# The first norm's weight: a partition-spreading DMA replaced by one row and two TensorE products

## The chip, the cores and the metric

The kernel runs on one core of one Trainium2 chip. The metric is the device time of the whole kernel in microseconds, the median of several runs. The lines of this document (L930 and so on) are lines of the kernel before, unless a sentence says that they are of the changed one.

## The reference

A conditioning vector `c` modulates two mixer layers, and two blocks with gated feed-forward layers follow. What matters here is the very start: the modulation and the norm of layer 0, ahead of the first projection.

```python
def adaln_norm(x, c, g, w_ada, b_ada):
    mod = jax.nn.silu(c) @ w_ada + b_ada
    shift, scale, gate = jnp.split(mod, 3, axis=-1)
    h = rms_norm(x, g) * (1.0 + scale[:, None, :]) + shift[:, None, :]
    return h, gate[:, None, :]
...
    for i in range(DEPTH):
        h, gate = adaln_norm(x, c, norm_g[i], ada_w[i], ada_b[i])
...
            y = nsa_mixer(h, nsa_w_in[j], ...)
```

`x` is 256 tokens by 1024, `c` is 1 by 1024, `g` is a row of 1024 and `w_ada` is 1024 by 3072, all float32. The rest (two mixers, the output projections, the feed-forward layers, further norms) isn't touched by the change.

## The kernel before

Each engine has its own block of instructions in a fixed order written by hand, and semaphores tie the blocks together. Tokens lie on the 128 partitions in two tiles (`NT = 2`); `x` and `tok` are 128 x 2 x 1024.

**The start.** SyncE issues the large loads from one queue, in this order: `x` (1 MB), the four halves of the first two blocks of `ada_w0` (1 MB each, tiles `early_111` to `early_114`, "early"), the first half of the first `nsa_w_in` item (716 KB, into `ring`), then further blocks as earlier ones are used. ScalarE issues two small loads at its start: `c`, and the identity matrix (64 KB, into `tab`). GpSimd sets constants, issues the load of vector 0 (`load_vec(0)`, the weight `norm_g[0]`), then the load of `ada_b` (12 KB, one row, into `mod0`).

`vecs` in HBM has one row of 1024 for each of eleven norm vectors. `load_vec(v)` copies row v to all 128 partitions with `partition_broadcast`: 512 KB written for 4 KB of data, into one of the two halves of the tile `vec`.

**Modulation, block by block.** `EARLY = (2, 0, 3, 1)`: TensorE makes four blocks of 512 columns of `silu(c) @ w_ada`, first half of scale, first half of shift, then the second halves. The weights are the moving operand, and `cb` (128 x 32, silu(c) in column 0) the stationary one. One block is two halves of four products (L1339), into four 32-partition strips of a PSUM bank. VectorE adds the bank to `mod0` (L2402), TensorE multiplies with `ones` to sum the partitions and spread the result to all 128 (L1350), and VectorE takes it: for a scale block as `(scale + 1) * g` (L2411, `scale_gain`, which reads `vec`), for a shift block in the last step of the norm (L2422). The normed tokens are transposed on TensorE (L528) into banks `T0`/`T1` and copied out as a high part (ScalarE, L538) and a low part (VectorE, L569). `keep_busy(n, ...)` (L1132) is n products without use, which TensorE works on while it would otherwise wait. From then on TensorE multiplies with split weights, high and low parts (`whi` from ScalarE, `wlo` from VectorE), in the three products of L1109 to L1111.

A float32 product of 128 x 512 shows in the trace as two MATMUL records; those of L1109 to L1111 show as one each.

Of the kernel before, what the change touches and what calls it, by code (L numbers as in the profile page):

```python
# [128 lines left out]
def two_stacks(nc, a, out):  # L129
    with ExitStack() as ctx:  # L130
        def sem(name):
            return ctx.enter_context(nc.semaphore(name))

        def stage(name, names):
            return Signals(ctx, nc, name, names)
# [5 lines left out]
        def sb(name, shape, dt=F32, over=None, skip=0):  # L141

            size = -(-4 * int(np.prod(shape[1:])) // 32) * 32
            if over is None:
                place[name] = at_byte[0]
                at_byte[0] += size
                assert at_byte[0] <= nc.sbuf_top, (name, at_byte[0], nc.sbuf_top)
            else:
                place[name] = place[over] + skip
            return nc.alloc_sbuf_tensor_at(name, list(shape), dt, offset=place[name])  # L150
# [32 lines left out]
        vec = sb("vec", [P, 2, D])  # L183
# [13 lines left out]
        ones = sb("ones", [P, P])  # L197
# [15 lines left out]
        TB = [ctx.enter_context(nc.psum_tensor(f"T{i}", [P, 512], F32)) for i in range(2)]  # L213
# [55 lines left out]
        vec_loaded, vec_used = [sem("vec0_loaded"), sem("vec1_loaded")], sem("vec_used")  # L269
# [3 lines left out]

        early_landed = [sem(f"early{m}_landed") for m in range(4)]
        near_landed, near_scaled = [sem("near0_landed"), sem("near1_landed")], sem("near_scaled")
        gains_loaded = sem("gains_loaded")
        early, late = stage("ada_early", "part summed full taken"), stage("ada_late", "part summed full taken")
        norm = stage("norm", "var rstd ready half resid squared meaned mean centered")
        turn = stage("turn", "turned taken low drawn")
# [188 lines left out]
        def plan_turn(name, groups, split=False):  # L468

            turns[name] = (groups, *turn_n, split)  # L470
            turn_n[0] += len(groups)
            turn_n[1] += sum(len(takes) for g, (_, takes) in enumerate(groups) if name not in SHARED or g % 2 == 0)
            turn_n[2] += len(groups) if split else 0
# [8 lines left out]
        def wait_turned(eng, name, upto=None):  # L482

            groups, _, t0, _, _ = turns[name]
            n = len(groups) if upto is None else upto
            eng.wait_ge(turn["taken"], t0 + (n + 1) // 2)
            eng.wait_ge(turn["drawn"], drawn0[name] + n // 2)

        def turned_all(name):

            groups, _, t0, l0, split = turns[name]
            return (turn["low"], l0 + len(groups)) if split else (turn["taken"], t0 + sum(len(takes) for _, takes in groups))
# [22 lines left out]
        def turn_pe(pe, name, ready=None, tile=None, only=None):  # L515
            groups, _, t0, l0, split = turns[name]
            for g, (srcs, takes) in of_tile(groups, tile) if only is None else ((only, groups[only]),):
                if ready is not None:
                    ready(g)
                if name in SHARED and g >= len(banks_of(name)):  # L520

                    free = (g - len(banks_of(name))) // 2 + 1
                    pe.wait_ge(*((turn["drawn"], drawn0[name] + free) if g % 2 else (turn["taken"], t0 + free)))
                elif name not in SHARED and g >= 2 and turn_bank(name, g) is turn_bank(name, g - 2):

                    pe.wait_ge(*((turn["low"], l0 + g - 1) if split else (turn["taken"], t0 + (g - 1) * len(takes))))
                for n, (src, width) in enumerate(srcs):
                    ins = pe.transpose(turn_bank(name, g)[0:width, n * P:(n + 1) * P], src, ident)  # L528
                ins.then_inc(turn["turned"], 1)
# [388 lines left out]
        def _(pool):  # L918
# [7 lines left out]
            def load_vec(v):  # L926
                if v >= 2:

                    pool.wait_ge(vec_used, v - 1)
                pool.dma_start(vec[:, v % 2, :], a["vecs"][v:v + 1, :].rearrange("a d -> (a d)").partition_broadcast(P)).then_inc(vec_loaded[v % 2], 16)  # L930
# [17 lines left out]
                    rotate(tl, dst[:, t, :].rearrange("p (h d) -> p h d", h=H), u[:, t, lo:lo + D].rearrange("p (h d) -> p h d", h=H),  # L948
                           cos, sin, H, HALF, t, scratch, ready)

            load_vec(0)
            pool.wait_ge(mod_zero, 1)
            pool.dma_start(mod0[0:1, :], a["ada_b"][0:1, :]).then_inc(mod0_loaded, 16)
            pool.wait_ge(consts_set, 4)
# [137 lines left out]
            load_vec(10)  # L1092
            rstd_of(8, 0)
            b_last = vec[:, 0, :]
            pool.wait_ge(vec_loaded[0], 16 * 6)

            pool.wait_ge(norm["centered"], 1)
            pool.wait_ge(norm["rstd"], 2 * 8 + 1)
# [8 lines left out]
        def _(pe):  # L1107
# [20 lines left out]
            def keep_busy(n, bank=None, src=None):  # L1128

                src = tab[:, 0:512] if src is None else src  # L1130
                for _ in range(n):
                    pe.matmul((S[0] if bank is None else bank)[:, 0:src.shape[1]], ident, src, start=True, stop=True)  # L1132
# [188 lines left out]
            def first_products(c, t, half, k0=0, k1=KT // 2):  # L1321

                pe.wait_ge(turn["low"], turns["h0"][3] + 2 * half + t + 1)
                pe.wait_ge(lo_done, part0["nsa_in"] + 2 * half + c + 1)
                wh, wl = (part[c][:, 0:KT * NSA_W].rearrange("p (k w) -> p k w", k=KT) for part in (whi, wlo))
                for k in range(half * KT // 2 + k0, half * KT // 2 + k1):
                    ins = split_products(G[2 * c + t][:, 0:NSA_W], hTh[:, k, t * P:(t + 1) * P], hTl[:, k, t * P:(t + 1) * P],
                                         wh[:, k, :], wl[:, k, :], k == 0, k == KT - 1)
                return ins
# [4 lines left out]
            for b in range(len(EARLY)):  # L1334
                bank = S[b % 2]
                for half in range(2):
                    pe.wait_ge(early_landed[2 * (b % 2) + half], 16 * (b // 2 + 1))
                    for k in range(ADA_K):
                        ins = pe.matmul(bank[32 * k:32 * k + 32, :], cb[:, half * ADA_K + k, :], early_raw[2 * b + half][:, k, :],  # L1339
                                        start=(half == 0), stop=(half == 1))  # L1340
                ins.then_inc(early["part"], 1)
                if b == 2:
                    first_products(0, 0, 0)
                elif b == 3:
                    first_products(1, 1, 0, 1, 3)
                else:
                    keep_busy(2, S[(b + 1) % 2], ident)
                pe.wait_ge(early["summed"], b + 1)
                at = EARLY[b] * ADA_W
                pe.matmul(early_bank[b][:], ones[:], mod0[:, at:at + ADA_W], start=True, stop=True).then_inc(early["full"], 1)  # L1350
                if b == 2:
                    first_products(0, 1, 0)
                    first_products(1, 1, 0, 0, 1)
                if b == 1:
                    keep_busy(4, S[(b + 1) % 2], ident)
                if b == 3:
                    first_products(1, 1, 0, 3, 4)
                    pe.wait_ge(vec_used, 1)
                    first_products(1, 0, 0, 0, 1)
                if b % 2 == 1:  # L1360
                    for t in range(NT):
                        pe.wait_ge(early["taken"], 2 * (b // 2) + t + 1)
                        turn_pe(pe, "h0", only=2 * (b // 2) + t)
                if b < 2:
                    keep_busy(4, S[(b + 1) % 2], ident)
# [3 lines left out]
            for m in range(NSA_C):  # L1369
# [19 lines left out]
                for i in {4: (0,), 5: (1,), 7: (2, 3)}.get(m, ()):  # L1389
                    pe.wait_ge(nsa_s["blocks"], 9)  # L1390
                    v, kh = i // 2, i % 2
# [4 lines left out]
                    for c in range(8):  # L1396
# [3 lines left out]
                                        start=(kh == 0 and c < 4), stop=(kh == 1 and c >= 4))  # L1400
# [278 lines left out]
        def _(sc_e):  # L1679
            tl = Tally(sc_e, act_step)  # L1680
            sc_e.dma_start(csil, a["c"]).then_inc(c_loaded, 16)
            sc_e.dma_start(ident, a["tables"][:, 0:P]).then_inc(ident_loaded, 16)
            sc_e.wait_ge(c_loaded, 16)
            sc_e.wait_ge(consts_set, 1)
            sc_e.activation(cb[:, :, 0], csil, ACT.Silu).then_inc(cb_ready, 1)
# [222 lines left out]
            def first_high(c, half):  # L1908

                if half == 0:  # L1910
                    sc_e.wait_ge(w1_early_landed[c], 16)
                else:
                    sc_e.wait_ge(*((w1_early_landed[0], 32), (landed[1], 16))[c])
                at = slice(half * NSA_HALF, (half + 1) * NSA_HALF)
                sc_e.copy(whi[c][:, at], ring[:, c, at]).then_inc(hi_done, 1)

            first_high(0, 0)
            for t in range(NT):
                turn_act(sc_e, "h0", only=t)
# [205 lines left out]
        def _(dve):  # L2125
# [36 lines left out]
            def next_vec():  # L2162
                v = vec_n[0]
                vec_n[0] += 1
                dve.wait_ge(vec_loaded[v % 2], 16 * (v // 2 + 1))
                return vec[:, v % 2, :]

            def scale_gain(mod):

                scale, g = mod[:, D:2 * D], next_vec()  # L2170
                done(STT(scale, scale, 1.0, g, ALU.add, ALU.mult), vec_used)
# [748 lines left out]
```

## Time and profile before

| | |
|---|---|
| median of 3 runs | 993.37 us (991.65 to 993.83) |
| the profiled execution, its own time | 991.93 us |
| its span, first to last instruction | 990.1 us |
| TensorE matmul busy | 956.0 us, 97% of the span |
| VectorE busy | 648.0 us, 65% |
| ScalarE busy | 471.7 us, 48% |
| GpSimd busy | 183.7 us, 19% |
| HBM read | 176.65 MB |
| mean granted TensorE clock | 0.996 |

The profiled execution's own time has 1.83 us outside the span. Times within it are counted from the span's start. Engines are PE (TensorE's products), PEld (its weight loads), DVE (VectorE), ACT (ScalarE), POOL (GpSimd) and SP (SyncE); a q behind an engine's name is its issuing of DMAs. In a row of the timeline the first number is the start, the second the length, and the bracket tells how long the engine sat idle before and for whom it waited.

### The profile page before, as it was taken

What the parts mean: (1) busy time and instruction counts of PE and PEld (TensorE: products, weight loads), DVE (VectorE), ACT (ScalarE), POOL (GpSimd) and SP (SyncE); (2) the same over time, 40 slices, a digit from 0 to 9 for tenths busy, and PEclk for the clock granted to TensorE, in tenths of its full rate; (3) what the DMA queues carried; (4) which work ended last, traced back from release to release, by engine and by line L of the source; (5) the groups of instructions that cost most, each with busy time, mean ns of one, the idle gap of its engine ahead of it and who ended that gap; (6) DMA issues with size and microseconds to landing.
All of it is one profiled execution on the core that took longest, in us unless ns stands there. A gap on an engine that the chain in (4) does not pass through costs nothing.

```text
span 990.1 us, 15100 instructions
## 1 busy us (share of the span) xinstructions
PE 956.0 (97%) x5656; PEld 806.9 (81%) x5656; DVE 648.0 (65%) x1164; ACT 471.7 (48%) x733; POOL 183.7 (19%) x154
## 2 busy tenths in 40 slices
PE   5999899899999999999999999999999999999996
PEld 2799666778886789988888888879999888888885
DVE  4656567875664775667767666676446776766666
ACT  1353577535545645573344444444457334444442
POOL 2015137403970401140000000010024000000001
PEclk9999999999999999999999999999999999999999
DMA  9955655434565247223365565534532336455541
GB/s 374 368 223 168 224 202 200 141 129 170 192 221 203 86 153 258 90 86 128 128 243 211 209 211 191 188 138 170 201 118 96 128 129 247 187 188 190 190 185 43
DMA packets 24104, 178.37 MB, mean 180 GB/s; under 512 B 3791, under 2 KB 4223, under 8 KB 7927
## 3 DMA queue, kind: packets, MB, share of 16 engines
q1 hardware_dynamic: 19840, 166.70, 45.3%
q0 software_dynamic: 2224, 8.94, 2.8%
q10 hardware_dynamic: 1991, 2.07, 0.8%
q8 instruction: 31, 0.51, 0.2%
q14 instruction: 18, 0.15, 0.0%
HBM read 176.65 MB, written 1.05 MB: 179 GB/s over the span
## 4 chain that ended last, share of the span: by engine, by line
PE 85%; DVE 9%; ACT 3%; DMA 2%; issue 1%; POOL 0%; SPq 0%; DVEq 0%; ACTq 0%
PE G L1109 15%; PE G L1111 14%; PE G L1110 14%; PE S L1229 8%; PE T L1229 8%; PE S L1228 4%; PE T L1228 3%; PE T L623 2%; PE T L528 2%; PE G L633 1%; PE G L632 1%; PE G L631 1%; DMA early<-in_ada_w 1%; PE G L441 1%; DVE wlo L2143 1%
## 5 line engine op out<-in xcount | busy, mean ns | idle before, releaser
L2277 DVE TENSOR_TENSOR wlo<-ring,whi 128x2048 fp32r<-128x2048 f32 x88 | 154.4, 1758 | 88.6 <-ACT whi L1845 54.0
L1109 PE MATMUL G<-whi,hTh 128*128 128x512 f32 (+3 forms) x560 | 197.0, 352 | 1.2 <-DVE oTl L569 0.9
L1110 PE MATMUL G<-wlo,hTh 128*128 128x512 f32 (+3 forms) x544 | 186.7, 343 | 0.0
L1111 PE MATMUL G<-whi,hTl 128*128 128x308 f32 (+3 forms) x496 | 167.3, 337 | 0.0
L2143 DVE TENSOR_TENSOR wlo<-ring,whi 128x1024 fp32r<-128x1024 f32 (+3 forms) x66 | 105.1, 1631 | 65.4 <-ACT whi L1703 65.2
L1229 PE MATMUL S<-hT,whi 128*128 128x512 f32 x336 | 122.1, 397 | 0.0
L1229 PE MATMUL T<-hT,whi 128*128 128x512 f32 x336 | 120.7, 394 | 0.0
L1109 PEld LDWEIGHTS G<-whi,hTh 128*128 128x128 f32 x560 | 105.5, 188 | 14.5 <-issue 2.8
L1110 PEld LDWEIGHTS G<-wlo,hTh 128*128 128x128 f32 x544 | 102.7, 189 | 8.0 <-issue 0.7
L1111 PEld LDWEIGHTS G<-whi,hTl 128*128 128x128 f32 x496 | 93.3, 188 | 5.7
L1840 ACT CAST whi<-ring 128x2048 fp32r<-128x2048 f32 x44 | 83.9, 1908 | 25.8 <-PE S L1309 17.4
L1703 ACT CAST whi<-ring 128x1024 fp32r<-128x1024 f32 (+3 forms) x66 | 75.1, 1186 | 43.4 <-PE G L1111 30.1
L1228 PE MATMUL S<-hT,wlo 128*128 128x256 f32 x294 | 82.6, 281 | 0.0
L1850 ACT ACTIVATE sil<-gsum 128x256 f32<-128x256 f32 x44 | 18.4, 418 | 132.4 <-DVE gsum L2298 132.4
L1228 PE MATMUL T<-hT,wlo 128*128 128x256 f32 x294 | 81.4, 277 | 0.0
L1229 PEld LDWEIGHTS S<-hT,whi 128*128 128x128 f32 x336 | 63.1, 188 | 13.8 <-DVE wlo L2277 0.6
L1229 PEld LDWEIGHTS T<-hT,whi 128*128 128x128 f32 x336 | 63.0, 187 | 11.0
L936 POOL TENSOR_TENSOR rstd<-var,mhalf 128x1 f32<-128x1 f32 x18 | 11.6, 648 | 320.7 <-DVE var L2155 229.3
L1109 PE MATMUL G<-whi,acth 128*128 128x512 f32 x176 | 68.8, 391 | 0.4 <-DVE actl L2307 0.4
L1111 PE MATMUL G<-whi,actl 128*128 128x512 f32 x176 | 68.5, 389 | 0.0
L1110 PE MATMUL G<-wlo,acth 128*128 128x512 f32 x176 | 68.5, 389 | 0.0
L1845 ACT CAST whi<-ring 128x1024 fp32r<-128x1024 f32 x44 | 46.2, 1050 | 29.8 <-PE G L1111 29.8
(380 smaller groups left out, 1839.8 us busy)
## 6 DMA issues: line engine op xcount, KB each, us to landing
ring<-in_ffn SPq DMA_DIRECT2D x44, 1536.0 KB, 6.4
ring<-in_dil_w_in SPq DMA_DIRECT2D x16, 1024.0 KB, 4.8
ring<-in_cd_w_in SPq DMA_DIRECT2D x10, 1232.0 KB, 5.3
ring<-in_ada_w SPq DMA_DIRECT2D x12, 1024.0 KB, 6.6
early<-in_ada_w SPq DMA_DIRECT2D x8, 1024.0 KB, 10.0
ring<-in_nsa_w_in SPq DMA_DIRECT2D x5, 1432.0 KB, 7.1
ring<-in_ab_w_in SPq DMA_DIRECT2D x4, 1440.0 KB, 6.3
vec<-in_vecs POOLq DMA_DIRECT2D x11, 512.0 KB, 5.5
```

Source lines behind the costliest of these rows:

```text
L528: ins = pe.transpose(turn_bank(name, g)[0:width, n * P:(n + 1) * P], src, ident)
L623: ins = pe.transpose(TB[j % 2][:, b * P:(b + 1) * P], scr[:, j % 4, 1 + b * P:1 + (b + 1) * P], ident)
L1109: pe.matmul(out_, act_h, w_h, start=first_, stop=False)
L1110: pe.matmul(out_, act_h, w_l, start=False, stop=False)
L1111: return pe.matmul(out_, act_l, w_h, start=False, stop=last_)
L1228: pe.matmul(bank[:, 0:T], wlo[b][:, at], hT2[:, k, 0, :], start=False, stop=False)
L1229: ins = pe.matmul(bank[:], whi[b][:, at], hT2[:, k, :, :].rearrange("p h t -> p (h t)"), start=(k == 0), stop=(k == KT - 1))
L1703: sc_e.copy(whi[(k0 + j) % 2][:, at], raw[:, at]).then_inc(hi_done, 1)
L1840: sc_e.copy(whi[b][:, gu], ring[:, b, gu]).then_inc(st["gu_hi"], 1)
L1845: sc_e.copy(whi[b][:, dn], ring[:, b, dn]).then_inc(st["dn_hi"], 1)
L2143: TT(wlo[k % 2][:, at], raw[:, at], whi[k % 2][:, at].bitcast(F32), ALU.subtract).then_inc(lo_done, 1)
L2277: TT(wlo[b][:, part], ring[:, b, part], whi[b][:, part].bitcast(F32), ALU.subtract).then_inc(st[what + "_lo"], 1)
```

## The change

Vector 0 is no longer spread to the partitions by a DMA of GpSimd. ScalarE issues, as its third DMA, a load of the one row (4 KB) into partition 0 of the same place in `vec`. TensorE multiplies it with one row of `ones` (one partition by 128) in two products of 512 columns, into `T0` and `T1`; they stand between the two halves of the first modulation block. ScalarE copies both banks over `vec`, ahead of its first cast of weights. `scale_gain` waits for these two copies and no longer for the DMA. Since GpSimd's loads of the first `vec` half are now one fewer, the counts waited for by later vectors are lowered by one load; those loads are as before.

```diff
@@ gpsimd
-            load_vec(0)
             pool.wait_ge(mod_zero, 1)
             pool.dma_start(mod0[0:1, :], a["ada_b"][0:1, :]).then_inc(mod0_loaded, 16)
...
-            pool.wait_ge(vec_loaded[0], 16 * 6)
+            pool.wait_ge(vec_loaded[0], 16 * 5)
@@ tensor
             for b in range(len(EARLY)):
                 bank = S[b % 2]
                 for half in range(2):
+                    if (b, half) == (0, 1):
+                        pe.wait_ge(gain_row, 16)
+                        for part in range(2):
+                            pe.matmul(TB[part][:], ones[0:1, :], vec[0:1, 0, part * 512:(part + 1) * 512], start=True, stop=True).then_inc(gain_spread, 1)
                     pe.wait_ge(early_landed[2 * (b % 2) + half], 16 * (b // 2 + 1))
@@ scalar
             sc_e.dma_start(csil, a["c"]).then_inc(c_loaded, 16)
             sc_e.dma_start(ident, a["tables"][:, 0:P]).then_inc(ident_loaded, 16)
+            sc_e.dma_start(vec[0:1, 0, :], a["vecs"][0:1, :]).then_inc(gain_row, 16)
             sc_e.wait_ge(c_loaded, 16)
...
+            sc_e.wait_ge(gain_spread, 2)
+            for part in range(2):
+                sc_e.copy(vec[:, 0, part * 512:(part + 1) * 512], TB[part][:]).then_inc(gain_spread, 1)
             first_high(0, 0)
@@ vector, next_vec
-                dve.wait_ge(vec_loaded[v % 2], 16 * (v // 2 + 1))
+                dve.wait_ge(*((vec_loaded[v % 2], 16 * ((v + 1) // 2)) if v > 0 else (gain_spread, 4)))
```

TensorE's order at its start, before the change; L1339 are the halves of the modulation blocks, L1350 the products with `ones`, L1132 the products without use.

```order
1 L1339 MATMUL S<-early_111,cb 32x512 x4
2 L1339 MATMUL S<-early_112,cb 32x512 x4
3 L1132 MATMUL S<-tab 128x128 x2
4 L1350 MATMUL G<-mod_77,ones 128x512
5 L1132 MATMUL S<-tab 128x128 x4
6 L1339 MATMUL S<-early_113,cb 32x512 x4
7 L1339 MATMUL S<-early_114,cb 32x512 x4
```

The same place in the changed kernel, whose lines from here on have other numbers (its L1342 is the L1339 of before, its L1353 the L1350).

```order
1 L1342 MATMUL S<-early_111,cb 32x512 x4
2 L1339 MATMUL T<-vec,ones 128x512 x2
3 L1342 MATMUL S<-early_112,cb 32x512 x4
4 L1131 MATMUL S<-tab 128x128 x2
5 L1353 MATMUL G<-mod_77,ones 128x512
6 L1131 MATMUL S<-tab 128x128 x4
7 L1342 MATMUL S<-early_113,cb 32x512 x4
```

Two products stand between the two halves of the first block, and everything behind keeps its order.

ScalarE's order at its start before the change: its two loads, the activation that makes `cb`, then the casts of the first weight items (L1915) and of the transposed tokens (L538).

```order
1 L1681 DMA small<-in_c 128x8
2 L1682 DMA tab<-in_tables 128x128
3 L1685 ACT_TABLE_LOAD
4 L1685 ACTIVATE cb<-small 128x8
5 L1915 CAST whi_58<-ring 128x1432
6 L538 CAST hTh<-T 128x4x128 x2
```

The same place in the changed kernel.

```order
1 L1684 DMA small<-in_c 128x8
2 L1685 DMA tab<-in_tables 128x128
3 L1686 DMA vec<-in_vecs 1x1024
4 L1689 ACT_TABLE_LOAD
5 L1689 ACTIVATE cb<-small 128x8
6 L1923 COPY vec<-T 128x512 x2
7 L1919 CAST whi_58<-ring 128x1432
```

One more DMA is issued ahead of the activation, and two copies out of PSUM stand ahead of the first cast.

## Rows read from the trace of the kernel before

**Rows 1.** The page: span, busy time of each engine, DMA by slice
```profile
span 990.1 us, 15100 instructions
PE 956.0 (97%) x5656; PEld 806.9 (81%) x5656; DVE 648.0 (65%) x1164; ACT 471.7 (48%) x733; POOL 183.7 (19%) x154
```
**Rows 2.** The chain that ended last, 0 to 80 us: start, length, what
```profile
1.76 10.81 DMA early<-in_ada_w
12.62 1.94 PE S L1339 x8
...
15.71 1.59 PE G L1350 x2
```
**Rows 3.** Timeline of PE, first 26 us
```profile
8.66 1.93 PE L1339 MATMUL S<-early,cb 128*32 128x512 f32 x8 [8.66 <-DMA early<-in_ada_w]
12.62 1.94 PE L1339 MATMUL S<-early,cb 128*32 128x512 f32 x8 [2.02 <-DMA early<-in_ada_w]
...
15.50 1.80 PE L1350 MATMUL G<-mod,ones 128*128 128x512 f32 x2
17.14 1.05 PE L1132 MATMUL S<-tab 128*128 128x128 f32 x8
18.12 1.92 PE L1339 MATMUL S<-early,cb 128*32 128x512 f32 x16
...
20.93 1.12 PE L1350 MATMUL G<-mod,ones 128*128 128x512 f32 x2 [0.24 <-DVE mod L2402]
...
25.04 1.92 PE L1339 MATMUL S<-early,cb 128*32 128x512 f32 x16
```
**Rows 4.** Timeline of SP: issues of the third and fourth load of ada_w
```profile
2.23 0.71 SPq L842 DMA_DIRECT2D early<-in_ada_w  x1
2.98 0.46 SPq L842 DMA_DIRECT2D early<-in_ada_w  x1
```
**Rows 5.** DMA issues, third and fourth load of ada_w: last number is us to landing
```profile
early<-in_ada_w SPq DMA_DIRECT2D x1, 1024.0 KB, 12.8
early<-in_ada_w SPq DMA_DIRECT2D x1, 1024.0 KB, 14.5
```
**Rows 6.** DMA issues, 0 to 13 us, small loads and vector 0
```profile
vec<-in_vecs POOLq DMA_DIRECT2D x1, 512.0 KB, 8.6
tab<-in_tables ACTq DMA_DIRECT2D x1, 64.0 KB, 6.7
...
mod<-in_ada_b POOLq DMA_DIRECT2D x1, 12.0 KB, 8.6
```
**Rows 7.** Timeline of the other engines, first 25 us
```profile
1.22 0.44 ACTq L1682 DMA_DIRECT2D tab<-in_tables  x1
...
3.86 0.73 POOL L930 DMA_DIRECT2D vec<-in_vecs  x1
...
14.72 0.69 DVE L2402 TENSOR_TENSOR mod<-mod,S 128x512 f32<-128x512 f32 x1 [4.60 <-PE S L1339]
...
17.34 0.69 DVE L2411 SCALAR_TENSOR_TENSOR mod<-G,vec 128x512 f32<-128x512 f32 x1 [1.93 <-PE G L1350]
...
19.29 1.39 ACT L1915 CAST whi<-ring 128x1432 fp32r<-128x1432 f32 x1 [15.80 <-DMA ring<-in_nsa_w_in]
...
23.53 1.31 ACT L538 CAST hTh<-T 128x512 fp32r<-128x512 f32 x2 [2.85 <-PE T L528]
```
**Rows 8.** Windows: length, busy of PE PEld DVE ACT POOL, PEclk, DMA, GB/s
```profile
10.60:12.60 2.00, 0.00 (x0) 0.00 (x0) 0.00 (x0) 0.00 (x0) 0.15 (x1) 1.00 1.03 389
27.00:60.00 33.00, 32.78 (x197) 29.52 (x198) 18.85 (x19) 14.21 (x17) 3.22 (x2) 1.00 0.94 367
191.00:194.40 3.40, 3.40 (x10) 2.58 (x9) 2.89 (x2) 0.00 (x0) 0.00 (x0) 0.50 0.56 229
```
**Rows 9.** Timeline of DVE and ACT, 50 to 60 us
```profile
51.56 3.21 DVE L2143 TENSOR_TENSOR wlo<-ring,whi 128x1432 fp32r<-128x1432 f32 x2 [2.21 <-ACT whi L1703]
...
56.17 0.46 ACT L1734 COPY u<-G 128x358 f32<-128x358 f32 x1 [3.00 <-PE G L1111]
```

More of the change, by code:

```diff
@@ L275, in two_stacks @@
         near_landed, near_scaled = [sem("near0_landed"), sem("near1_landed")], sem("near_scaled")
-        gains_loaded = sem("gains_loaded")
+        gains_loaded, gain_row, gain_spread = sem("gains_loaded"), sem("gain_row"), sem("gain_spread")
         early, late = stage("ada_early", "part summed full taken"), stage("ada_late", "part summed full taken")
```

## Prediction

> **What bounds the kernel now.** I read the page first: TensorE is busy for 956.0 of 990.1 us, the next engine for 648.0 [rows 1]. The change touches only the first tens of microseconds, so I then took the chain that ended last over that stretch. It begins with a load of `early`, 10.81 us long, and from 12.62 on it is almost only TensorE [rows 2]. The timelines show each wait. TensorE works on the first half of the first modulation block from 8.66 to 10.59, then waits 2.02 us for the second half, which lands at about 12.6, and works on that until 14.56 [rows 3]. From there to the third block at 25.04 the only wait in its rows is the 0.24 us for VectorE, because products without use fill the gaps [rows 3]. From 27 to 60 us it is busy for 32.78 of 33.00 [rows 8]. What TensorE gains or loses at the start is therefore passed on, unless a load is late at the new time.
>
> Three neighbours matter. The DMA engines are full in TensorE's wait, 389 GB/s [rows 8]. The load of vector 0 is issued at 3.86 and lands 8.6 later, at 12.5, just when the late half lands [rows 6, 7]. And the first work of TensorE runs at half rate: 8 records of L1339 take 1.93 us at 8.66, 16 of the same take 1.92 at 18.12; one product of L1350 takes 1.80 at 15.50 and 1.12 at 20.93 [rows 3]. The step lies near 17.1, where eight records of L1132 already take only 1.05. That is 4.5 us after work without a pause began at 12.62. The clock column reads 1.00 over the stretch in rows 8, so here I go by the durations; the low level that the column does show, 0.50 (1.2 of 2.4 GHz) from 191.0 to 194.4, ends after 3.4 us in which TensorE was busy throughout [rows 8].
>
> **Removed: the spreading load.** It writes 512 KB. At 389 GB/s that is 1.35 us of all DMA engines. The loads of `ada_w` say the same in another way: landings at 8.66, 12.62, then 2.23 + 12.8 = 15.0 and 2.98 + 14.5 = 17.5, so steps of 4.0, 2.4 and 2.5 us, and the long one is 1.5 longer, where the vector's load ran beside it [rows 3 to 5]. I take 1.4. So the second half lands at about 11.2, the fourth at 16.1, and what is queued behind them comes about 1.4 earlier as well: the first ring load at 17.9 where ScalarE now sees it at 19.29 [rows 7].
>
> GpSimd's load of `ada_b` was issued 0.73 later than it could have been and landed 8.6 after, at 13.2; it now starts at 3.86 with nothing before it. VectorE needs it at 14.72, behind TensorE, so this gives nothing [rows 6, 7].
>
> **Added: the load of the row.** ScalarE issues it third, at 1.66, for 0.44 as its neighbour [rows 7]. That pushes `cb` by 0.44, to about 4 us; TensorE needs it at 8.66: nothing. When does the row land? The trace has no load of 4 KB at this place. The nearest is the identity, 64 KB, on the same queue just ahead: 1.22 + 6.7 = 7.9 [rows 6, 7]. The row should follow it shortly; TensorE asks for it at 10.6. I take no wait. The far end is the load of 12 KB, 8.6 from its issue though it stood behind the vector: 1.66 + 8.6 = 10.3, still no wait.
>
> **Added: two products on TensorE.** They stand between the halves. A product of 512 columns costs 1.80 at half rate and 1.12 alone at full rate, some 0.9 in a row of them [rows 3]. Two at half rate: 3.6, from 10.6 to 14.2. The products have one partition of depth, where all rows of before have 128, so their cost is not in the trace; below it is bounded by zero, above by 3.6, and I take the price of the row with the same columns.
>
> (TensorE: Matmul & The Clock Gate, of the Trainium skill, section "Why this matters for your kernels", says that a matmul of small depth alone takes as long as a full one. By that page it is the upper price, 3.6 and not zero, which speaks against the change: the work is longer than the 2.02 us of wait that it falls into. No row here shows such a product.)
>
> **What it does to the chain.** Without the step in rate: products until 14.2, second half until 16.1, where it was 14.56. But the pause that TensorE had from 10.6 to 12.6 is gone, it works from 8.66 on, and the rate should step up earlier. With the same 4.5 us as in rows 3 that is 13.2. Of 3.6 + 1.93 = 5.5 us of half-rate work from 10.6, 2.6 is then done and 2.9 left, which takes 1.45: the block is done at 14.65, 0.1 later than before. VectorE adds it (0.16 + 0.69, rows 7), L1350 starts at about 15.55 and now takes 1.12, not 1.80: it ends at 16.67 where it ended at 17.30. The second block follows as before 0.82 later, at 17.5 and not 18.12, and its load has landed at 16.1. Sum: +0.1 and -0.7, net **-0.6 us**.
>
> **Added on ScalarE.** Two copies of 128 x 512 out of PSUM, 0.65 each by rows 7 (1.31 for two casts), from about 14 to 15.5. ScalarE has nothing there: it waits 15.80 us for the ring [rows 7]. VectorE asks for the result at L2411, 17.34 before and 16.7 after: covered by over 1 us. Without that cover the 1.3 would stand on the chain.
>
> **Does the rest follow?** The third block starts at 25.04 without a wait [rows 3]; 0.6 earlier is less than the 1.4 by which its loads move. Later, VectorE has the first half of the low part for the fourth item ready at 51.56 + 1.6 = 53.2, TensorE takes it at about 56.1, when ScalarE takes the chunk before it [rows 9]: 2.9 us to spare. So I expect the 0.6 to stay until the end.
>
> **Bounds.** If the rate steps up after 3.4 us of work as at 191 [rows 8], it does so at 12.1: 1.5 done, 4.0 left in 2.0, block done at 14.1, net -1.2. If the two products cost nothing, the second half runs from its landing at 11.2 to about 13.1, and the second block is bound by its own load at 16.1 or 16.2: -1.9. If the rate steps up no earlier than before, at 17.1, the block is done at 16.1, L1350 runs from 17.0 to 18.1, net +0.8.
>
> **Against the median.** The sum is made against the profiled execution, 991.93, of which 1.83 lies outside the span. That is 1.4 below the median of the runs, 993.37, which are 2.2 apart. The net should hold for either: 991.3 for one like the profiled, and 993.37 - 0.6 = 992.8 for the median, my prediction. Differences under 0.2%, 2.0 us, are about what a measurement of this kernel can't tell from no change.
>
> **Rivals.**
> 1. *No change that shows* (my forecast): -1.2 to +0.8 around -0.6. Chance 0.78, together with the case that TensorE's rate steps up no earlier.
> 2. *The DMA relief comes through whole.* The first block was held by a load, the loads move by 1.4, the products turn out near free, and the earlier full rate comes on top: -1.9 by the bound above, about 991.5. For: the wait of 2.02 and the full DMA engines [rows 3, 8]. Against: the products have the columns of rows that cost 1.80. To pass the 2.0 it needs a little more than the bound, or the scatter of the runs. Chance 0.11.
> 3. *A wait for the row takes the place of the wait removed*, slower. TensorE's queue is in order: behind the wait for the row stand its two products, the second half and all else, and SyncE waits for the block's end to issue the next loads. If the row doesn't overtake what SyncE has queued, it lands not at 8 but with them. Landing with the load that comes at 11.2 costs 0.6 more than the forecast, no net change; landing with the fourth at 16.1: products at full or half rate 1.8 to 3.6, second half 1.0 to 1.9, block done at 18.9 to 21.6, thus +4.3 or more, about 998 and above. It turns into a measurable loss from a landing near 13 on. For: the third and fourth of SyncE's loads of `ada_w` needed 12.8 and 14.5 us to land [rows 5]. Against: the identity, 16 times the bytes, issued only 0.44 earlier, landed at 7.9. Chance 0.11, with the scatter on that side.
>
> (DMA: Bandwidth & Descriptors, of the Trainium skill, section "Queues, rings and completion order", states that an engine serves the queues with work in turn, packet by packet. By that rule the row waits for what ScalarE queued, not for SyncE's loads, and the last rival falls; the landing of the identity agrees.)
>
> **Chances and range.** Faster 0.11, within 0.2% 0.78, slower 0.11. The range takes the bounds -1.9 to +0.8, and some 0.5 to either side for the scatter of the runs (a quarter of their 2.2): 991.0 to 994.7.
>
> **What would show the steps.** In the profile after: the wait of 2.02 at 12.62 gone; two products (four records) on bank T right behind the first half, 0.8 to 0.9 each record at first; the half behind them with records of half the length or a mix; L1350 near 1.1; the second block at about 17.5; the ring load seen by ScalarE near 17.9; two copies on ScalarE before it. The prediction is wrong if TensorE waits for the row before its products, if the products take far less than 0.4 a record, if L1350 still takes 1.8, or if a wait for a load appears between 20 and 60 us and takes the gain back.

## The result, and the profile after

The changed kernel is slower: 994.54 us (median of 14 runs, 992.91 to 995.91) against 993.45 us (14 runs, 990.59 to 994.47), ratio 1.0017 with a 95% interval of 1.0009 to 1.0025. That is +1.7 us (0.9 to 2.5) where -0.6 was forecast. The ratio isn't the quotient of the two medians, which lie 1.1 us apart; differences in time are taken from the ratios from here on. A second measurement of the same two kernels gave 1.0025 (1.0013 to 1.0036). The profiled execution took 992.91 us, its span is 991.1.

TensorE's timeline after, first 27 us, answers to [rows 3]; L1342 are the halves of the modulation blocks, L1339 the two new products, L1353 the old L1350.

```profile
9.06 1.94 PE L1342 MATMUL S<-early,cb 128*32 128x512 f32 x8 [9.06 <-DMA early<-in_ada_w]
...
10.93 3.78 PE L1339 MATMUL T<-vec,ones 1*128 1x512 f32 x4
...
14.63 1.94 PE L1342 MATMUL S<-early,cb 128*32 128x512 f32 x8
...
17.52 1.39 PE L1353 MATMUL G<-mod,ones 128*128 128x512 f32 x2
...
19.72 1.92 PE L1342 MATMUL S<-early,cb 128*32 128x512 f32 x16
...
26.63 1.92 PE L1342 MATMUL S<-early,cb 128*32 128x512 f32 x16
...
28.49 0.43 PE L1108 MATMUL G<-whi,hTh 128*128 128x358 f32 x1
```

The wait of 2.02 us is gone, and none for the row has come: the products follow the first half directly. But they take 3.78, the second half behind them still takes 1.94 for eight records, which is half rate, and L1353 with 1.39 straddles the step from half rate to full rate. (As in the kernel before, the clock column of the profile reads 1.00 over this stretch, so the rate is read from the durations.) The first block ends at 16.57 where it ended at 14.56, the second starts at 19.72 where it started at 18.12. From there everything is 1.6 us later: the third block at 26.63 and not 25.04.

The other engines after, same stretch, answer to [rows 7].

```profile
1.69 0.54 ACTq L1686 DMA_DIRECT2D vec<-in_vecs  x1
...
14.74 1.07 ACT L1923 COPY vec<-T 128x512 f32<-128x512 f32 x2 [10.90 <-PE T L1339]
...
16.74 0.69 DVE L2409 TENSOR_TENSOR mod<-mod,S 128x512 f32<-128x512 f32 x1 [6.67 <-PE S L1342]
...
18.19 1.39 ACT L1919 CAST whi<-ring 128x1432 fp32r<-128x1432 f32 x1 [2.37 <-DMA ring<-in_nsa_w_in]
```

The loads did come earlier: ScalarE sees the first ring load at 18.19 and not 19.29. Nothing on TensorE's path was waiting for the earlier landings any more.

### The profile page after: what moved, and what is told of

Read it like the earlier page. It is cut to its first block, busy times and chain, and to the rows that moved or that the text cites. A ratio compares the mean times of both kernels' runs of the same rounds, so it can differ in the third digit from the quotient of the medians.

```text
span 991.1 us, 15110 instructions
## 1 busy us (share of the span) xinstructions
PE 958.8 (97%) x5660; PEld 808.1 (82%) x5660; DVE 647.7 (65%) x1164; ACT 472.0 (48%) x735; POOL 183.1 (18%) x153
## 3 DMA queue, kind: packets, MB, share of 16 engines
HBM read 176.13 MB, written 1.05 MB: 179 GB/s over the span
## 4 chain that ended last, share of the span: by engine, by line
PE 84%; DVE 10%; ACT 2%; DMA 2%; issue 1%; POOL 0%; DVEq 0%; SPq 0%; ACTq 0%
PE G L1108 14%; PE G L1110 14%; PE G L1109 14%; PE S L1228 8%; PE T L1228 8%; PE S L1227 4%; PE T L1227 3%; PE T L623 2%; PE T L528 2%; PE G L633 1%; PE G L632 1%; PE G L631 1%; DVE wlo L2150 1%; PE G L441 1%; PE S L1342 1%
```

## Experiments

Each time stands against runs of the kernel before on the same chip, 11 runs of the kernel to 33 of before. "First product" is the start of the first product of the first projection in the profile, 26.89 before and 28.49 after; it shows what the start did in that one execution. Lines of the experiments shift by a few; their roles are named. "Depth" is the number of partitions that a product sums over: 1 in the two new products, 128 elsewhere at the start.

Three explanations of the loss stood against each other, and the expectations call them by letters. Theory A: products of small depth don't bring on the step to full rate. Theory B: the moment of the step only scatters between executions. Theory C: the two products are simply longer than the wait they fall into, and the rate has no part.

**b_plus_depth1 and b_plus_depth128: the products by themselves.** The kernel before with two products between the halves; only the depth differs.

```diff
                 for half in range(2):
+                    if (b, half) == (0, 1):
+                        for part in range(2):
+                            pe.matmul(TB[part][:], ones[0:1, :], early_raw[0][0:1, part, :], start=True, stop=True)
@@ the second kernel instead
+                            pe.matmul(TB[part][:], ones[:], early_raw[0][:, part, :], start=True, stop=True)
```

> The kernel before, spreading load kept, with two products of one partition of depth (128 x 512, on data that has landed) between the halves of the first block; their result is not used. It shows what the products cost by themselves. Theories A and C: they take 3.7 us from 10.6 to 14.3 against a wait of 2.0, so +1.6 to +1.8 us against before, as much as the changed kernel loses: there the relief of the DMA engines then bought nothing, since TensorE was no longer waiting for the load. If products of one partition counted for the clock: +0.0 to +0.6.

> As b_plus_depth1, but the two products have 128 partitions of depth. Theory A: the rate steps up between 12 and 15.5 us, -0.6 to +0.4 us against before, and 1.5 to 2 us less than b_plus_depth1. Theories B and C: no difference between the two, both +1.6 to +1.8.

Depth 1: ratio 1.0021 (1.0011 to 1.0030), +2.1 us. Depth 128: 1.0003 (0.9994 to 1.0012), +0.3 us. TensorE's timeline with depth 1:

```profile
10.48 3.78 PE L1339 MATMUL T<-early,ones 1*128 1x512 f32 x4
14.19 1.94 PE L1342 MATMUL S<-early,cb 128*32 128x512 f32 x8
...
17.07 1.78 PE L1353 MATMUL G<-mod,ones 128*128 128x512 f32 x2
```

and with depth 128:

```profile
10.46 2.62 PE L1339 MATMUL T<-early,ones 128*128 128x512 f32 x4
13.01 1.06 PE L1342 MATMUL S<-early,cb 128*32 128x512 f32 x8
...
14.99 1.13 PE L1353 MATMUL G<-mod,ones 128*128 128x512 f32 x2 [0.27 <-DVE mod L2405]
```

The same four records of the same width, at the same place, on data of the same tile. At full depth the rate steps up within them, and the second half and L1353 run at full rate; at depth 1 all of it stays at half rate until within L1353, behind 18. First product at 28.43 and 25.70. The products at depth 1 alone, added to the kernel before with its 512 KB load still there, cost as much as the changed kernel loses.

**c_depth128, c_depth64, c_depth32: the same question in the changed kernel.** Vector 0 holds sums of `ada_w` here, the norm's weight is left out.

```diff
-                            pe.matmul(TB[part][:], ones[0:1, :], vec[0:1, 0, part * 512:(part + 1) * 512], start=True, stop=True).then_inc(gain_spread, 1)
+                            pe.matmul(TB[part][:], ones[:], early_raw[0][:, part, :], start=True, stop=True).then_inc(gain_spread, 1)
@@ c_depth64 (and 32)
+                            pe.matmul(TB[part][:], ones[0:64, :], early_raw[0][0:64, part, :], start=True, stop=True).then_inc(gain_spread, 1)
```

> The changed kernel, in which the two products have all 128 partitions of depth (ones, 128 x 128, times 128 x 512 of the first half of the ada_w load that has just been used), so that vector 0 holds sums of ada_w and not the norm's weight. Number, width and place of the products are the same. Theory A (depth): products of one partition don't count as work for TensorE's clock; with full depth the rate steps up 2 to 4 us earlier than in the changed kernel, the second half of the first block or L1353 runs at full rate, and the kernel is about 2 us faster than the changed one, -0.3 to -1.0 us against the one before. Theory B (the moment of the step only scatters from one execution to the next, and depth has no part in it): as the changed kernel, +1 to +2 us against before. Theory C (the products are simply longer than the wait they fall into, and the clock has no part): also as the changed kernel, +1.6, with the step where it was.

> As c_depth128, but the two products read 32 partitions. It asks whether only the depth of one fails to hold the clock. If any depth above one counts: as c_depth128, -0.3 to -1.5 us against before. If the work counts by the share of the array that it uses: as the changed kernel, +1 to +2.

> As c_depth32, with 64 partitions. If the work counts by the share of the array: between the two, or on the side of c_depth128, -1.5 to +1.5 us against before.

Depth 128: 0.9991 (0.9981 to 1.0001), -0.9 us. Depth 64: 1.0019 (1.0009 to 1.0029). Depth 32: 1.0024 (1.0013 to 1.0035). TensorE in c_depth128:

```profile
10.47 3.32 PE L1339 MATMUL T<-early,ones 128*128 128x512 f32 x4
13.72 1.06 PE L1342 MATMUL S<-early,cb 128*32 128x512 f32 x8
```

With 64 and 32 partitions the products take 3.78 and 3.77 and the second half 1.93, as with one. So it isn't that one partition is a special case: of the depths run, only the full one brought the step forward. Between 64 and 128 none was run. Depth 64 lost 1.9 us, more than the 1.5 that its expectation allowed. The interval of c_depth128 just includes no change; it lies wholly below both intervals of the changed kernel.

The profile of c_depth128 shows one thing more. VectorE's first row behind the norm's sums reads:

```profile
14.99 0.69 DVE L2409 TENSOR_TENSOR mod<-mod,S 128x512 f32<-128x512 f32 x1 [4.89 <-ACT vec L1923]
```

It waited for ScalarE's copies, not for TensorE: the wait stands in `next_vec`, ahead of the adding of the bank, and not at the operation that reads the vector. Here this cost next to nothing, since TensorE's second half ended at 14.78, only 0.2 before; but the copies now sit at the edge of the chain.

**c_no_load: what the removal of the load is worth.** No row, no products, no copies; GpSimd fills vector 0 with ones, so the norm's weight is left out.

```diff
+            pool.memset(vec[:, 0, :], 1.0).then_inc(gain_spread, 1)
...
-            sc_e.dma_start(vec[0:1, 0, :], a["vecs"][0:1, :]).then_inc(gain_row, 16)
@@ and the two products and the two copies are taken out
```

> The changed kernel without the row's load, without the two products and without the two copies; GpSimd fills vector 0 with ones instead, so the first norm's weight is left out. It shows what the removal of the 512 KB load is worth by itself. If the relief is real: the second half of the first block lands at 11.2 to 11.6 and the block is done at 13.2 to 13.6, the kernel is 1.0 to 1.4 us faster than before. If the loads are held by something else: 0.

0.9986 (0.9977 to 0.9995), -1.4 us. TensorE's timeline:

```profile
8.67 1.93 PE L1339 MATMUL S<-early,cb 128*32 128x512 f32 x8 [8.67 <-DMA early<-in_ada_w]
...
11.28 1.94 PE L1339 MATMUL S<-early,cb 128*32 128x512 f32 x8 [0.67 <-DMA early<-in_ada_w]
...
14.16 2.04 PE L1350 MATMUL G<-mod,ones 128*128 128x512 f32 x2
15.99 1.67 PE L1132 MATMUL S<-tab 128*128 128x128 f32 x8
17.59 1.92 PE L1339 MATMUL S<-early,cb 128*32 128x512 f32 x16
```

The second half's load lands at 11.28 and not 12.62: the 1.34 us are real. But in this profile they don't reach the projection whole. TensorE stays at half rate through L1350 (2.04) and most of L1132 (1.67, where 1.05 is full rate), so the step is at about 17.2, where it was before; the second block starts only 0.5 earlier, and the first product too (26.35). That the time measured agrees with 1.34 is therefore not explained by the rows. The end of its span, 990.1, says little, since this execution had a longer stretch at half clock in the middle of the kernel (below).

**b_one_busy: the rate by itself.** The kernel before, with one product of full depth in the wait.

```diff
+                    if (b, half) == (0, 1):
+                        pe.matmul(TB[0][:], ones[:], early_raw[0][:, 0, :], start=True, stop=True)
```

> The kernel before, spreading load kept, with one product of full depth (128 x 512, result not used) between the halves of the first block: 1.8 us of work in the wait of 2.0, so it delays nothing. It shows what keeping TensorE at work there is worth by itself. Theory A (work of full depth counts for the clock, the wait breaks it): the rate steps up between 11.8 and 15.3 us and not at 16 to 19, -0.5 to -1.5 us against before. Theory C (the clock has no part): 0.

0.9993 (0.9984 to 1.0002): -0.7 us, within the expected range but not clear of no change; the medians are 0.1 apart the other way. In its profile the second half starts at 12.86 with 1.23 and L1352, which is the L1350 of before, takes 1.12; first product at 25.73. The earlier step shows in the rows; that it earns time isn't shown.

**c_zero_rows and c_zero_split: the change made with full depth.** Both compute all of the reference. GpSimd sets the vector to zero, the row is loaded into partition 0, the products take all 128 partitions; VectorE waits where it reads. In the second, one product stands between the halves and the other replaces four products without use.

```diff
+            pool.memset(vec[:, 0, :], 0.0).then_inc(gain_row, 1)
...
-                            pe.matmul(TB[part][:], ones[0:1, :], vec[0:1, 0, part * 512:(part + 1) * 512], start=True, stop=True).then_inc(gain_spread, 1)
+                            pe.matmul(TB[part][:], ones[:], vec[:, 0, part * 512:(part + 1) * 512], start=True, stop=True).then_inc(gain_row, 1)
...
+                dve.wait_ge(gain_taken, b // 2 + 1)
                 done(STT(part, early_bank[b][:], 1.0, gain0[:, cols], ALU.add, ALU.mult), vec_used if b == 2 else None)
@@ c_zero_split, behind L1353 of the first block, for keep_busy(4)
+                if b == 0:
+                    pe.matmul(TB[1][:], ones[:], vec[:, 0, 512:1024], start=True, stop=True).then_inc(gain_row, 1)
```

> The changed kernel with the whole computation kept, and the spreading products at full depth: GpSimd sets vector 0 to zero, ScalarE loads the row into partition 0 behind its activation, and the products multiply all 128 partitions with a full 128 x 128 of ones. VectorE waits for the copies only ahead of L2418, the operation that reads them. Theory A: -0.6 to -1.3 us against before, about 2.5 less than the changed kernel. Theory B (scatter): as the changed kernel, +1.7.

> As c_zero_rows, but only the first of the two products stands between the halves; the second takes the place of the four products without use behind L1353 of the first block, since VectorE needs the second half of the vector only two blocks later. Theory A: 1.9 us or less between the halves, the first block done at 13.3 to 14.3, then bound by the load of the second block, which lands at about 16.2: -1.3 to -2.2 us against before. If the products' length were no part of the loss: as c_zero_rows.

c_zero_rows 0.9992 (0.9981 to 1.0002), c_zero_split 0.9992 (0.9983 to 1.0001); first product at 26.32 and 25.33. TensorE in c_zero_split:

```profile
10.57 2.08 PE L1339 MATMUL T<-vec,ones 128*128 128x512 f32 x2
12.57 1.16 PE L1342 MATMUL S<-early,cb 128*32 128x512 f32 x8
...
14.65 1.13 PE L1353 MATMUL G<-mod,ones 128*128 128x512 f32 x2 [0.28 <-DVE mod L2413]
15.62 1.02 PE L1368 MATMUL T<-vec,ones 128*128 128x512 f32 x2
...
16.57 1.92 PE L1342 MATMUL S<-early,cb 128*32 128x512 f32 x16
```

In both, the vector is zero but for one partition, and the step still came forward, so what decides is the depth that the product is given, not how much of the data is other than zero. The first product in the profile of c_zero_split comes 1.6 us before that of the kernel before, but the measured time only shows 0.8, under the 1.3 to 2.2 expected. Neither version's time is clear of no change, and the two can't be told apart by it.

**c_late_halves: keep the spreading load, move it.** All is computed; no products.

```diff
+                if b == 1:
+                    sp.dma_start(vec[:, 0, 0:512], a["vecs"][0:1, 0:512].rearrange("a d -> (a d)").partition_broadcast(P)).then_inc(gain_row, 16)
                 if b == 1 or b == 2:
                     sp.dma_start(ring[:, b - 1, 0:NSA_HALF], a["nsa_w_in"][b - 1][:, 0:NSA_HALF]).then_inc(w1_early_landed[b - 1], 16)
+                if b == 1:
+                    sp.dma_start(vec[:, 0, 512:1024], a["vecs"][0:1, 512:1024].rearrange("a d -> (a d)").partition_broadcast(P)).then_inc(gain_spread, 16)
```

> No products for the vector: it is spread by DMA as before, but in two halves of 256 KB on SyncE's queue, behind the fourth load of ada_w and behind the first ring load. The second half of the first block lands at 11.3 as in c_no_load, the first half of the vector at about 16.8, and VectorE has to spare until 19.6. Theories A and C: as c_no_load, -1.0 to -1.5 us against before. If 512 KB of spreading load cost wherever they stand: 0.

0.9987 (0.9978 to 0.9996), -1.3 us, with no work added. This is clearly faster than the changed kernel; against the kernel before it is little more than the 0.9 that two measurements of that one kernel differ by (below), and the medians are 0.6 apart. Timeline of PE and DVE:

```profile
9.18 3.86 PE L1342 MATMUL S<-early,cb 128*32 128x512 f32 x16 [9.18 <-DMA early<-in_ada_w]
12.97 0.71 PE L1135 MATMUL S<-tab 128*128 128x128 f32 x4
...
15.91 1.92 PE L1342 MATMUL S<-early,cb 128*32 128x512 f32 x16
17.50 0.69 DVE L2416 SCALAR_TENSOR_TENSOR mod<-G,vec 128x512 f32<-128x512 f32 x1 [3.60 <-DMA vec<-in_vecs]
...
19.80 0.69 DVE L2406 TENSOR_TENSOR mod<-mod,S 128x512 f32<-128x512 f32 x1
20.55 1.13 PE L1353 MATMUL G<-mod,ones 128*128 128x512 f32 x2 [2.07 <-DVE mod L2406]
```

Both halves of the first block run without a pause, and the products behind them are at full rate from 12.97 on. The second block starts 2.2 us before that of [rows 3], but VectorE sits idle for 3.60 until the vector has landed. The products it also needs, L1353, end at 15.08, so some 2.4 of that are the vector's. TensorE then waits 2.07 for VectorE, and 0.4 is left of the gain at 20.55 (20.93 before); the first product comes at 26.51. The vector half stands too late in the queue for this; an order with it ahead of the fourth load was not tried.

**before_again and after_again: the scatter.**

> The kernel before once more, for a second profile of it: what scatters between two executions. Theory A: its first block waits for the load as in rows 3, ends at 14.4 to 15.0, and the rate steps up at 16.0 to 19.4 us. Time as before, 0 +- 1 us.

> The changed kernel once more, for a second profile of it. Theory A: the four records of the products take 3.7 to 3.8 us at half rate again, and the rate steps up only after the first block's second half has begun at 14.2 to 14.7, at 17.6 us or later. Theory B: in some other execution the rate steps up within the products. Time +1 to +2.4 us against before.

The kernel before against itself: 1.0009 (0.9999 to 1.0019), so 0.9 us is what this measurement can show for nothing. The gains of 0.7 to 1.4 us over the kernel before, above, are hardly more; the losses of 1.7 to 2.5 with shallow products are. In the second profile of the kernel before L1350 takes 1.50 instead of 1.80 and the first product comes at 26.55. The changed kernel: 1.0025 (1.0013 to 1.0036). Its second profile has the products and the second half as in the first:

```profile
10.98 3.78 PE L1339 MATMUL T<-vec,ones 1*128 1x512 f32 x4
...
14.69 1.94 PE L1342 MATMUL S<-early,cb 128*32 128x512 f32 x8
```

Five profiles with products of less than full depth (after, after_again, b_plus_depth1, c_depth32, c_depth64) have the second half at half rate; the five with full depth (c_depth128, b_plus_depth128, b_one_busy, c_zero_rows, c_zero_split) have it at full rate or across the step. That the moment of the step merely scatters (theory B) is out by this and by the times: five measurements with shallow products lie at +1.7 to +2.5, the five with full depth at -0.9 to +0.3. It does scatter: by an estimate from the row in which the rate changes it lies at 18.3 to 19.9 in the five shallow profiles and at 16.4 and 17.1 in the two of the kernel before. Within each group the first product in the profile doesn't rank the times. That the products' length is all of it (theory C) is out by the pair b_plus_depth1 and b_plus_depth128: number, width and place are equal.

## Why the prediction was wrong

The step that failed is the one under "What it does to the chain": that the pause was gone, TensorE "works from 8.66 on, and the rate should step up earlier". It was gone, and the rate didn't. The sum put the step at 13.2; in the changed profile it falls within L1353, behind 18. The products of one partition keep TensorE busy in the profile but did not bring the step forward; the same products at full depth did (1.8 us between b_plus_depth1 and b_plus_depth128 by ratio). I had asked of the depth only what it costs, not what it does for the rate. The 4.5 us of work before the step that the sum took over from rows 3 were no constant either: by the rows in which the rate changes it was about 5.9 in c_no_load, counted from 11.28, and 3.8 in c_late_halves, counted from 9.18.

- *The removed load, 1.4 us*: right. In c_no_load the second half's load lands 1.34 earlier. In the changed kernel this bought nothing, since TensorE reached that half only at 14.63 and didn't wait for it. The first ring load came 1.1 earlier than before (18.19 against 19.29), where 1.4 was reckoned.
- *The row's load, no wait*: right; the products start behind the first half without a wait. The third rival fell: the row had landed by 10.93, while SyncE's later loads were still on their way. The Trainium skill (DMA: Bandwidth & Descriptors, "Queues, rings and completion order") has a DMA engine serve the queues that hold work in turn, packet by packet, and the trace agrees with that.
- *Products 3.6 at half rate*: 3.78, right in size. The 1.80 it was taken from wasn't wholly at half rate: that row straddles the step, and one product alone takes 2.04 where all of it is at half rate (c_no_load). Depth didn't change the cost: 3.78, 3.77 and 3.78 for 1, 32 and 64 partitions. The Trainium skill (TensorE: Matmul & The Clock Gate, "Why this matters for your kernels") says that a product of small depth alone takes as long as a full one, and the trace agrees.
- *The bound without an earlier step, +0.8*: the mechanism that happened, mis-sized. In the changed profile the second block starts 1.6 later. Of the 0.8 between, 0.3 to 0.4 is the first load, at 9.06 and not 8.66. What sets that is open: it is 9.12 in the second profile of the changed kernel, but 8.61 in c_depth128, which has the same loads, and 8.97 in b_one_busy, which has those of before. About 0.3 is L1353 with 1.39 where 1.12 was reckoned, the step lying later still (beyond 18, where the bound had 17.1), and 0.1 to 0.2 the products.
- *ScalarE's copies, covered*: right here (done at 15.81, VectorE at 16.74), but I put VectorE's wait at L2411, and it stands ahead of L2402. Where the products are quicker, as in c_depth128, that wait shows, though it costs under 0.1.
- *The rest follows*: right. The third block is 1.6 later, like the second, and the time measured, +1.7, is the same size. The two profiled spans differ by 1.0 only, but those of the second pair of profiles by 1.8 (991.5 and 989.7), with the third block 2.0 later. So the 1.0 of the first pair is no sign that 0.6 was won back on the way.

The time, 994.54, lies within the range of 991.0 to 994.7, and the loss is under the 2.0 us that the prediction called hard to tell from no change. Neither speaks for the mechanism. The direction was wrong, the range reached up that far only by a bound of +0.8 that was too small and 0.5 for scatter, and with 14 runs a side the measurement tells the loss from no change.

## What to carry to other kernels

Work put into a gap in which TensorE waits while still at half rate should use all partitions: here such products brought the step forward (that this beats leaving the gap empty isn't clear from the times), while shallow ones took the same time, delayed what is behind them, and gave nothing back. Ask of a load whether it stands ahead of something that is waited for; moving it behind that (c_late_halves, -1.3 us) did better than replacing it by compute (+1.7 us). A wait put where a value is fetched, and not where it is read, is a second path to check before adding a producer.

## What the runs showed of the hardware

In these runs the depth of the products decided when TensorE's rate stepped up: with four records of 512 columns over 3.8 us the rate stayed at half for 1, 32 and 64 partitions and stepped up within them for 128 (2.62, 2.89 and 3.32 us for the four in b_plus_depth128, c_zero_rows and c_depth128). With c_zero_rows the data were nearly all zeros.

The stretch at half clock in the middle, 3.4 us long in [rows 8], is about twice that in 5 of the 14 profiles (b_one_busy, c_depth32, c_depth64, c_no_load, c_zero_split). Windows of c_zero_split, TensorE alone (length, busy, granted clock, DMA share, GB/s):

```profile
187.00:193.70 6.70, 5.57 (x15) 0.50 0.46 159
193.70:197.00 3.30, 3.30 (x18) 1.00 0.91 318
```

5.57 us of work at 1.2 of 2.4 GHz there, against 3.40 in rows 8, is by an estimate from these two rows about 1 us of the execution's time. That is as large as what was looked for here, and one reason why single spans don't rank these kernels.
